# Head-by-head normalization, gating and rounded split of a delta-rule output inside its state scan

## The reference, cut to what matters

```python
def rms_norm(x, g):
    y = xf * lax.rsqrt(jnp.mean(xf * xf, axis=-1, keepdims=True) + EPS)
    return (y * g).astype(x.dtype)
...
    def step(S, inp):                       # chunked state scan, 4 chunks of 64 and two directions
        q_i, k_i, u_i, w_i, g_i, a_i = inp
        v_new = u_i - w_i @ S
        o = (q_i * exp(g_i)) @ S + a_i @ v_new
        S = S * exp(g_last) + (k_i * exp(g_last - g_i)).T @ v_new
...
    o_l, o_c = bidirectional_deltanet(...)
    def merge(glu, z, br, o, rows_):
        y_conv = conformer_conv(glu, ...)
        o = rms_norm(o, dn_norm_g) * jax.nn.silu(z)      # per head: mean over its 128 channels
        y_dn = o @ w_dn_out
        g_conv, g_dn = jnp.split(jax.nn.sigmoid(br), 2, axis=-1)
        return (g_conv * y_conv + g_dn * y_dn) @ w_out
```

## Time and profile before

| what | value |
|---|---|
| time, median of 3 runs | 4574.76 us (4574.54 to 4574.93) |
| profiled execution, its time | 4570.76 us |
| its span, first to last instruction | 4568.6 us |
| PE busy | 4327.2 us, 95% of the span |
| DVE busy | 2795.9 us, 61% |
| ACT busy | 1817.7 us, 40% |
| POOL busy | 207.1 us, 5% |
| granted TensorE clock, mean | 0.972 of full speed |

### The profile page before, as it was taken

One profiled execution on the slowest core, in us unless ns is written; L12 is line 12 of the kernel. 1 busy time (PEld: TensorE's weight loads), 2 busy tenths in 40 slices (PEclk: granted clock), 3 DMA queues, 4 the chain that ended last, 5 costly groups with the idle time before them and its releaser, 6 DMA issues. The chain is left out here.

```text
span 4568.6 us, 75234 instructions
## 1 busy us (share of the span) xinstructions
PE 4327.2 (95%) x28694; PEld 3782.1 (83%) x28694; DVE 2795.9 (61%) x4719; ACT 1817.7 (40%) x2650; POOL 207.1 (5%) x530
## 2 busy tenths in 40 slices
PE   8799999998999895999999999999999899999999
PEld 1595444677898895989999999888888799999999
DVE  0447877476579456545776666555555566765746
ACT  0331000252573333444444555444444455454534
POOL 0000000000000660000000000000000000210000
PEclk9899999998999997999999999999999899999999
DMA  8256555235786531545665555666666454444454
GB/s 334 96 175 240 229 221 221 91 117 185 266 270 203 148 111 66 182 167 190 206 207 183 179 176 176 210 217 216 214 214 215 150 190 174 149 157 148 167 194 157
DMA packets 211443, 846.31 MB, mean 185 GB/s; under 512 B 67521, under 2 KB 105761, under 8 KB 122145
## 3 DMA queue, kind: packets, MB, share of 16 engines
q1 hardware_dynamic: 211232, 843.37, 53.0%
HBM read 792.85 MB, written 50.45 MB: 185 GB/s over the span
## 5 line engine op out<-in xcount | busy, mean ns | idle before, releaser
L283 DVE TENSOR_TENSOR rounded<-arena,rounded 128x1024 fp32r<-128x1024 f32 x320 | 391.9, 1226 | 412.9 <-ACT rounded L276 412.8
L2245 PE MATMUL bank<-rounded,rounded 128*128 128x256 f32 x2048 | 590.8, 288 | 2.7 <-DVE rounded L2370 2.7
L2247 PE MATMUL bank<-rounded,rounded 128*128 128x256 f32 x2048 | 579.8, 283 | 0.0
L2246 PE MATMUL bank<-rounded,rounded 128*128 128x256 f32 x2048 | 579.7, 283 | 0.0
L3000 PE MATMUL bank<-rounded,rounded 128*128 128x256 f32 x1856 | 533.5, 287 | 10.1 <-DVE rounded L3247 6.2
L276 ACT ACTIVATE rounded<-arena 128x1024 fp32r<-128x1024 f32 x320 | 339.2, 1061 | 506.5 <-PE bank L2583 389.7
L3002 PE MATMUL bank<-rounded,rounded 128*128 128x256 f32 x1856 | 525.6, 283 | 0.0
L3001 PE MATMUL bank<-rounded,rounded 128*128 128x256 f32 x1856 | 525.6, 283 | 0.0
L198 PE MATMUL bank<-arena 128*128 128x512 f32 x1024 | 444.7, 596 | 1.3 <-PEq L326 1.3
L3247 DVE TENSOR_TENSOR rounded<-arena,rounded 128x1024 fp32r<-128x1024 f32 x232 | 292.4, 1260 | 240.6 <-ACT rounded L3047 240.0
L2298 ACT ACTIVATE rounded<-arena 128x1024 fp32r<-128x1024 f32 x256 | 270.9, 1059 | 422.4 <-PE bank L2247 421.5
(11 more groups left out here) (463 smaller groups left out, 9616.9 us busy)
## 6 DMA issues: line engine op xcount, KB each, us to landing
arena<-in_w_in SPq DMA_DIRECT2D x244, 1024.0 KB, 4.8
arena<-in_peer_u SPq DMA_DIRECT2D x128, 1024.0 KB, 5.0
arena<-in_peer_v SPq DMA_DIRECT2D x128, 1024.0 KB, 4.8
arena<-in_w_mod SPq DMA_DIRECT2D x96, 1024.0 KB, 6.7
arena<-in_w_out SPq DMA_DIRECT2D x40, 1024.0 KB, 4.7
arena<-in_w_conv_out SPq DMA_DIRECT2D x16, 1024.0 KB, 4.8
arena<-in_w_dn_out SPq DMA_DIRECT2D x16, 1024.0 KB, 4.8
arena<-in_peer_w_q SPq DMA_DIRECT2D x16, 1024.0 KB, 5.8
```

Of the source, the lines that this page charges most:

```text
L283: dve.tensor_tensor(k.staged(1, q), k.raw(r % 2)[:, c], k.staged(0, q), ALU.subtract).then_inc(k.lo_done, 1)
L2245: pe.matmul(out, wh, hi(kt), start=(kt == 0), stop=False)
L2246: pe.matmul(out, wh, lo(kt), start=False, stop=False)
L2247: mm = pe.matmul(out, wl, hi(kt), start=False, stop=(kt == KT - 1))
```

## The change

The stages "onorm" and "split_o" are gone. Their work for one head is spread over the scan: square on ACT (`squares`), sum on PE (`norm_sums`), root on ACT (`roots`), reciprocal on DVE (`inverse`), gain and gate (`gate`), product (`normalize`), high part on ACT (`high`), low part on DVE (`low`). Head h-1 is squared, summed, rooted and inverted during head h, and multiplied and split during head h+1. What is left of heads 14 and 15 runs after the last head. The sums take a tenth place in the ring of PSUM banks, and some waits of PE are exchanged for it. The Sigmoids and Silus move to `delta_prepare`: those of the delta gates become the function of the evacuation, the others are eight activations of four slots in the halves 66 to 80. DVE's products y times gate move from heads 5 to 8 to heads 1 to 4. The high parts of o go to slots 80 to 95, whose keys have been used by then, and the output stage's buffers trade places for it.

```diff
 delta_prepare, ACT
-                act.copy(k.t(slot_of(j), 1)[:, 0, :], k.ps[j % 4][:, 0:L]).then_inc(k.tile_out, 1)
+                act.activation(k.t(slot_of(j), 1)[:, 0, :], k.ps[j % 4][:, 0:L],
+                               ACT.Sigmoid if j >= 32 else ACT.Copy).then_inc(k.tile_out, 1)
+            def gates(q):
+                act.wait_ge(k.tile_out, e0 + 4 * q + 4)
+                x = k.t(slot_of(4 * q), 4)
+                act.activation(x, x, ACT.Sigmoid if q < 4 else ACT.Silu)
...
                 if i % 2 and i > 1:
                     evacuate(i // 2 - 1)
+                if i % 2 == 0 and 64 < i < 82:
+                    gates(i // 2 - 33)
 delta_scan
+    USES = 10
-    W0, W1, X5, T0, T1, Y5, Z5, X6, Z6 = range(9)
+    W0, W1, X5, T0, T1, Y5, Z5, X6, N, Z6 = range(10)
+    sums = lambda h: k.ps[4 + (USES * (h + 1) + (N if h + 1 < HEADS else W0)) % 4][:, 0:L]
-        return bank(4 + (9 * n + use) % 4)
+        return bank(4 + (USES * n + use) % 4)
 PE
             def x5_(n):
-                if n >= 1:
-                    pe.wait_ge(x6_kept, n)
+                if n >= 3:
+                    pe.wait_ge(rooted, n - 2)
+                elif n >= 1:
+                    pe.wait_ge(vtok_done, n)
             def z5_(n):
+                pe.wait_ge(x5_kept, n + 1)
             def z6_(n):
-                pe.wait_ge(vtok_done, n + 1)
+                pe.wait_ge(y5_kept, n + 1)
             def w_(h):
-                pe.wait_ge(y5_kept, h + 1)
+                pe.wait_ge(x6_kept, h + 1)
+            def norm_sums(h):
+                pe.wait_ge(squared, h + 1)
+                if h + 2 < HEADS:
+                    pe.wait_ge(vtok_done, h + 3)
+                if h == HEADS - 1:
+                    pe.wait_ge(rooted, h)
+                pe.matmul(sums(h), k.ones[:], square, start=True, stop=True).then_inc(summed, 1)
...
                 if after:
                     x6_(h + 1)
+                if h > 0:
+                    norm_sums(h - 1)
                 new(h, 3)
...
+            norm_sums(HEADS - 1)
 ACT
-            def gates(n): ...
+            def squares(h):
+                act.wait_ge(o_kept, 2 * (h + 1))
+                if h > 0:
+                    act.wait_ge(summed, h)
+                act.activation(square, o(h), ACT.Square).then_inc(squared, 1)
+            def roots(h):
+                act.wait_ge(summed, h + 1)
+                if h > 0:
+                    act.wait_ge(normed, h)
+                act.activation(root, sums(h), ACT.Sqrt, bias=k.eps[:, 0:1], scale=1.0 / P).then_inc(rooted, 1)
+            def high(h):
+                act.wait_ge(normed, h + 1)
+                act.activation(k.r(hi_slot + h, 1)[:, 0, :], o(h), ACT.Copy).then_inc(o_high, 1)
...
                 vnew(h, 0)
+                if h > 0:
+                    squares(h - 1)
                 x5_out(n); vnew(h, 1); values(n)
-                if h < 12:
-                    gates(h)
+                if h > 1:
+                    high(h - 2)
                 vnew(h, 2); z5_out(n); x6_out(n)
+                if h > 0:
+                    roots(h - 1)
                 vnew(h, 3)
...
+            squares(HEADS - 1); high(HEADS - 2); roots(HEADS - 1); high(HEADS - 1)
 DVE
+            def inverse(h):    waits rooted:           dve.reciprocal(root, root)
+            def gate(h):       waits squared:          o(h) = o(h) * dn_g * z(h)    (scalar_tensor_tensor)
+            def normalize(h):  waits inverted, gated:  o(h) = o(h) * root           (tensor_tensor)
+            def low(h):        waits o_high:           r(lo_slot+h) = o(h) - r(hi_slot+h)
...
                 w_kept_(h)
                 new_state(h, 0)
+                if h > 1:
+                    normalize(h - 2)
+                if h > 0:
+                    gate(h - 1)
                 scaled(n, ksc[n % 2], k.kdec, ksc_done)
                 new_state(h, 1)
                 y5_out(n); scaled(n, kneg, k.negegc, kneg_done)
+                if h > 1:
+                    low(h - 2)
                 new_state(h, 2)
                 z5_out(n); z6_out(n)
                 outputs(h)
-                if 5 <= h < 9: y *= gate, after gate_done
+                if h > 0:
+                    inverse(h - 1)
+                if 1 <= h < 5: y *= gate
+            normalize(HEADS - 2); gate(HEADS - 1); low(HEADS - 2); inverse(HEADS - 1)
+            normalize(HEADS - 1); low(HEADS - 1)
 output_stage, program
-    M_HI, M_LO, X1, T_HI, T_LO, SQ, Q = 80, 64, 96, 32, 48, 112, 64
+    M_HI, M_LO, X1, T_HI, T_LO, SQ, Q, KEYS = 96, 64, 80, 32, 48, 112, 64, 104
-        delta_scan(k, 48, 112, 128, 64, scratch)
-        channel_norm(k, "onorm", ...)
-        split(k, "split_o", 160, 176, 160)
+        delta_scan(k, 48, 112, 128, 80, 160, scratch)
-        output_stage(k, (...), 176, 160, 64, 48, 32, u[0:2], x1_saved)
+        output_stage(k, (...), 80, 160, 64, 48, 32, u[0:2], x1_saved)
```

More of the change, by code:

```diff
@@ L1521, in delta_prepare, with delta_scan @@
     k.evacs += tiles
-def delta_scan(k, y_slot, gate_slot, z_slot, br_slot, scratch):
+def delta_scan(k, y_slot, gate_slot, z_slot, hi_slot, lo_slot, scratch):
     nc = k.nc
@@ L1553, in delta_scan @@
     S, O = (0, 1), (2, 3)
-    W0, W1, X5, T0, T1, Y5, Z5, X6, Z6 = range(9)
+    o = lambda h: k.t(lo_slot + h, 1)[:, 0, :]
+    square, root = k.t(194, 1)[:, 0, :], k.t(195, 1)[:, 0, :]
+    W0, W1, X5, T0, T1, Y5, Z5, X6, N, Z6 = range(10)
+    sums = lambda h: k.ps[4 + (USES * (h + 1) + (N if h + 1 < HEADS else W0)) % 4][:, 0:L]
     def side(n, use):
-        return bank(4 + (9 * n + use) % 4)
+        return bank(4 + (USES * n + use) % 4)
     def ahead(n, use):
@@ L1575, in delta_scan @@
             "n5_set", "n6_set", "d5_set", "r5_set", "d6_set", "r6_set", "invt_set"))
-        tr_ready, ksc_done, kneg_done, vtok_done, w_ready, o_ready, o_kept, gate_done, gated = (sem(n) for n in (
-            "turned", "k_scaled", "k_negated", "v_kept", "w_ready", "o_ready", "o_kept", "gates_done", "gated"))
+        tr_ready, ksc_done, kneg_done, vtok_done, w_ready, o_ready, o_kept, gated = (sem(n) for n in (
+            "turned", "k_scaled", "k_negated", "v_kept", "w_ready", "o_ready", "o_kept", "gated"))
+        squared, summed, rooted, inverted, o_gated, normed, o_high, o_low = (sem(n) for n in (
+            "o_squared", "o_summed", "o_root", "o_root_inverted", "o_gated", "o_normed", "o_high", "o_low"))
         o_ready2 = sem2("o_state_read")
@@ L1868, in _ @@
                     z6_out(n)
+            squares(HEADS - 1)
+            high(HEADS - 2)
+            roots(HEADS - 1)
+            high(HEADS - 1)
         @block.vector
@@ L1923, in outputs, with inverse, gate, normalize @@
                 for c in range(2):
-                    dve.tensor_copy(k.t(160 + h, 1)[:, 0, c * P:(c + 1) * P], bank(O[c])[:, 0, :]).then_inc(o_kept, 1)
+                    dve.tensor_copy(o(h)[:, c * P:(c + 1) * P], bank(O[c])[:, 0, :]).then_inc(o_kept, 1)
+            def inverse(h):
+                dve.wait_ge(rooted, h + 1)
+                dve.reciprocal(root, root).then_inc(inverted, 1)
+            def gate(h):
+                dve.wait_ge(squared, h + 1)
+                dve.scalar_tensor_tensor(out=o(h), in0=o(h), scalar=k.col("dn_g"), in1=k.t(z_slot + h, 1)[:, 0, :],
+                                         op0=ALU.mult, op1=ALU.mult).then_inc(o_gated, 1)
+            def normalize(h):
+                dve.wait_ge(inverted, h + 1)
+                dve.wait_ge(o_gated, h + 1)
+                dve.tensor_tensor(o(h), o(h), root, ALU.mult).then_inc(normed, 1)
+            def low(h):
+                dve.wait_ge(o_high, h + 1)
+                dve.tensor_tensor(k.r(lo_slot + h, 1)[:, 0, :], o(h), k.r(hi_slot + h, 1)[:, 0, :],
+                                  ALU.subtract).then_inc(o_low, 1)
             for b in range(2):
@@ L1947, in _ @@
                 outputs(h)
-                if 5 <= h < 9:
-                    q = h - 5
+                if h > 0:
+                    inverse(h - 1)
+                if 1 <= h < 5:
+                    q = h - 1
                     if q == 0:
                         dve.wait_ge(y_in, 16)
-                    dve.wait_ge(gate_done, q + 1)
                     dve.tensor_tensor(k.t(y_slot + 4 * q, 4), k.t(y_slot + 4 * q, 4), k.t(gate_slot + 4 * q, 4),
                                       ALU.mult).then_inc(gated, 1)
+            normalize(HEADS - 2)
+            gate(HEADS - 1)
+            low(HEADS - 2)
+            inverse(HEADS - 1)
+            normalize(HEADS - 1)
+            low(HEADS - 1)
 def elementwise(k, name, ops):
@@ L3764, in program @@
                       scratch)
-        delta_scan(k, 48, 112, 128, 64, scratch)
[L3766 to L3769, removed]
-        split(k, "split_o", 160, 176, 160)
+        delta_scan(k, 48, 112, 128, 80, 160, scratch)
         u, v = i["peer_u"], i["peer_v"]
```

(4 more changed lines are left out.)

2 lines of the change are left out of this document (1 added, 1 removed).

## The result

The changed kernel took 4526.97 us (median of 4 runs, 4526.26 to 4536.0) against 4574.85 us (4 runs, 4574.54 to 4577.17): ratio 0.9899, 95% interval 0.9882 to 0.9916, 47.9 us less. Forecast were 37.9 less, 4536.9, with 4530 to 4551 as the range. So the sign was right, the gain 10 us larger than forecast, and the time lies 3 us under the range.

What follows compares the result with a forecast made beforehand. PE, busy 95% of the span, was taken to bound the kernel, with a serial DVE norm behind the scan. -49.7 + 7.1 + 4.4 + 0.3 + 0 = -37.9 us, from a median of 4574.76 to 4536.9; range 4530 to 4551.

Steps and rivals of the forecast that it cites:

- What goes: Between the scan's last output copy and the output stage's first matmul: 59.4 us go, 9.7 return, 49.7 won.
- The tail of 9.7: Serial work behind the last head, with the next stage's start up to PE's first matmul: 9.7 us come back.
- The sums: PE between `x6_` and `new(h, 3)`, no idle time there: 15 heads pay 0.475 each, 7.1 us; bounds 0 and 11.4.
- The reciprocal: DVE before `w_kept_`: 1.71 us just fits the idle gap, within 0.02; cost 0, bounds 0 and 1.0 a head.
- Late in every head: Rival: semaphore hand-overs delay `w_kept_` by 0.3 to 1.0 us in 15 heads; 4541 to 4552 us, chance 0.13.
- The y products: DVE in heads 1 to 4, behind the reciprocal and uncovered: 1.1 us each, 4.4 us; bounds 0 and 4.9.
- the root's load: ACT in head 1: one table load of 1.28 us for the root, mostly covered; 0.3 us, bounds 0 and 1.3.
- The preparation: ACT in `delta_prepare`: eight activations and nine table loads fit; cost 0, or 20 us if nothing were covered.
- blocked switches: Rival: a function switch blocks ACT for twice the load in the Silu stretch; 8.5 us, 4545 us, chance 0.05.
- loads round the root: Rival: root and copy in different sets, a load before and behind each head's root; 25 us, 4562, chance 0.04.
- Slower: Rival: added idle moments bring PE's clock down inside the scan; 49.5 us, 4586 us, chance 0.04.
- more is won: Rival: y products find cover (4.4) and the output stage starts at full clock (1.6); 4531 us, chance 0.04.

Runs made afterwards that it cites:

- sums_twice: The changed kernel with each head's sum matmul issued twice, the second signalling; one time, 4534.63 us.
- sums_rounded: The changed kernel with squares and ones written as fp32r, so a sum is one PE record; 4529.77 us, ratio 0.9905 to the kernel before.
- y_covered: The changed kernel with the y product of heads 1 to 4 issued between `z5_out` and `z6_out`; 4529.97 us, ratio 0.9909 to the kernel before.
- gates_prep: The kernel before with only the Sigmoids and Silus moved from the scan to the preparation; 4576.44 us, ratio 1.0005.
- dve_more: The changed kernel with one more DVE copy of 128x128 behind the reciprocal; one time, 4531.11 us.

## Why the prediction was right in its terms and missed the time

- **What goes, 49.7.** Measured 49.45, the last head's sum included. The tail of 9.7 was 9.6, and the output stage's first matmul lasts 0.58 us as before, at half clock (granted 0.50 from 1750.3 to 1753.6), as forecast.
- **The sums, 7.1.** 0.44 a head instead of 0.475: 6.2 in the 14 whole periods, and the last in the tail. sums_twice and sums_rounded show it twice more, as 0.43 added and 0.32 removed.
- **The reciprocal, 0.** Right, and with at least 0.13 us of room that the reading had not seen. "Late in every head" is refuted: the plain heads have the sum's 0.44 and nothing else.
- **The y products, 4.4, and the root's load, 0.3.** Measured 3 x 0.95 + 1.34 = 4.2 us for both, against 4.7; 0.39 of the 1.34 is the load's delay. The size of each product was taken 0.15 too long (1.1 for 0.95). y_covered takes 4.0 out.
- **The preparation, 0.** Right; gates_prep shows the nine loads and eight activations free, and that the scan gains nothing. The rivals "blocked switches" and "loads round the root" (one load at L1880) are refuted. "Slower" too: the clock stays at 1.00 over the scan.

These add up to -49.4 + 10.3 = -39.1 in the first pair, where the prediction had -37.9. So the mechanism was right, and the terms were off by 1.2 us together. The other 8.8 of the 10 us that the time was missed by lie in two terms that the prediction gave no width. It held all other stages at the one profile's times, that is at 0: they differed by 2.9 + 1.1 - 0.5 + 1.0 = 4.5 us in the first pair, with another 0.4 outside the spans. And it added "the median of the runs is 4.0 us above it" as a fixed offset of the median over the profiled execution: that offset was 0.3 after the change, 3.8 less than the 4.1 of before.

The step that failed is the range built on this: "the bounds of the y products and of the sums: -6, +6", "4531 to 4543", and with the rival "more is won" a low end of 4530. It holds only what the edits may cost and leaves out how far the median of a few executions lies from the next median, although the prediction's own sum names 9 us as about what a measurement can tell from no change. The -6 and +6 aren't the bounds of the terms either: 0 to 11.4 for the sums and 0 to 4.9 for the y products give -11.5 and +4.8. A low end of 4525.4 would have held the time, but for a wrong reason, since neither the sums nor the y products were free.

What the runs showed in its place: three times within 0.4 us looked like a fixed offset, but 41 times of the same kernel have a standard deviation of 4.7 us, and the medians of three comparisons of the changed kernel lie at 4526.97, 4531.35 and 4537.64. The first of them is the lowest; in the other two the gain was 37.6 and 38.7, and both medians lie inside 4531 to 4543. That the scored time fell outside was chance in part, and a forecast of 37.9 so close to these two gains is partly luck as well. A mean of four executions with a deviation of 5.1 us is itself uncertain by 5.1 / 2 = 2.6 us, their median by a little more. The median of the three runs that gave 4574.76 adds 4.7 / sqrt(3) = 2.7 us or a little more, the two together some 3.7, and the range had to be that much wider at both ends at least.

What stays open: the 3 us between 42.1 and 38.9, which may be chance, and what makes the granted clock and the waits for DMAs in `conv_stage` differ from one execution to the next. Whether sums placed in spare columns of a bank already in use, with the ring of nine kept, would save anything wasn't tried.

## What to carry to other kernels

A serial stage of a secondary engine between two stages that PE bounds can give back most of its length if its pieces fit the engines' idle time in a repeating loop: here 49 of 59 us went, and 10 came back as longer periods. Check each piece against the idle time directly in front of the instruction it displaces, not against busy shares: 1.2 us in a gap of 1.7 was free alone and cost 0.95 a head once a reciprocal stood in the same gap, and moving it ahead of `z6_out` brought 4 us back. Sum the effect in the stages where it acts, and take the range from that sum and from the spread of whole executions, for which three close times are no measure.

## What the runs showed of the hardware

- An instruction's duration isn't its price: a 128x256 f32 matmul with ones lasts 0.60 us in its two records and delays what follows by 0.43 to 0.44; as fp32r one record of 0.36, price 0.12.
- A short DVE copy of 0.16 us behind a reciprocal starts 0.08 before the latter's recorded end, and the next copy starts 0.11 behind its start (dve_more).
- A reciprocal of 128x256 f32 on DVE takes 1.71 to 1.75 us, a product of the same size 0.42.
- Function table loads at 1.28 us each, nine of them in some 49 us, cost no time where ACT otherwise waited about 2 us a half for PE.
- The same code under a PE busy all the time was granted 0.68 in one execution and 0.94 in another, in the same 20 us of its span. The stage took 5.9 us longer in the former; 2.6 of them are PE's busy time and 3.3 its idle time.
